# A two-block network kernel: states of the recurrence advanced from PSUM, the branch's gate a chunk ahead, and the moments' sums in PSUM

## The reference

```python
hx = modulate(rmsnorm(x, g_pre_mix[i]), sh1, sc1)
yx = token_mixers(hx @ w_in[i], s_f, s_b, rows, GRID_W, *gla_p, g_head[i], w_sc[i], b_sc[i])
x = x + gt1 * rmsnorm(yx @ w_out[i], g_post_mix[i])
hx = modulate(rmsnorm(x, g_pre_ffn[i]), sh2, sc2)
x = x + gt2 * rmsnorm(conv_ffn(hx, ...), g_post_ffn[i])

# token_mixers: a gated linear attention, forward and backward in time, beside a short convolution
o_gla = rmsnorm(o_f + o_b, g_head).reshape(bsz, t, GLA_WIDTH) * jax.nn.silu(og)
o_sc = sb * dwconv_row(sc * sx, w_sc, b_sc, rows, width)
return jnp.concatenate([o_gla, o_sc], axis=-1)

# one step of the recurrence of o_f and o_b
s_new = s * jnp.exp(b_last)[..., None] + jnp.einsum('bjhk,bjhv->bhkv', kc * jnp.exp(b_last[:, None] - b), vc)
```

## Time and profile before

| what | value |
|---|---|
| three executions | 1440.09, 1440.62, 1445.21 us |
| the profiled execution | 1444.85 us |
| its span | 1443.1 us |
| busy: TensorE, weight load, VectorE, ScalarE, GpSimd | 96%, 78%, 64%, 27%, 58% |
| TensorE's idle time | 59.8 us (span less 1383.3) |
| mean granted clock of TensorE | 0.972 of full speed |

### The profile page before, as it was taken

The page is one execution under the profiler, slowest core; times in us unless marked ns, Lnnn a source line. Parts: engine busy times, 40 slices in busy tenths (PEclk is TensorE's granted clock), DMA queues, the critical chain, the costliest instruction groups (busy, mean ns, idle before and its releaser), DMA issues.

```text
span 1443.1 us, 19746 instructions
## 1 busy us (share of the span) xinstructions
PE 1383.3 (96%) x6947; PEld 1123.8 (78%) x6947; DVE 929.6 (64%) x1305; ACT 391.7 (27%) x751; POOL 832.0 (58%) x651
## 2 busy tenths in 40 slices
PE   6999899989899999999999999999899999999998
PEld 4677678877788888888877888666688888888887
DVE  5696687756677777774038698735766888886000
ACT  3442223332222222201013202345413333332000
POOL 1343434425666666677746676432367777777775
PEclk9999999989799999999989999999999999999999
DMA  9456222112133333254322333211133333333332
GB/s 355 150 199 210 56 58 60 59 45 73 42 90 102 94 95 102 86 164 140 95 83 74 88 102 88 60 58 45 43 90 88 102 94 95 101 90 94 92 93 84
DMA packets 224459, 142.05 MB, mean 98 GB/s; under 512 B 5611, under 2 KB 211088, under 8 KB 224400
## 3 DMA queue, kind: packets, MB, share of 16 engines
q1 hardware_dynamic: 221333, 136.45, 31.7%
q10 hardware_dynamic: 3067, 4.78, 1.0%
HBM read 139.12 MB, written 2.10 MB: 98 GB/s over the span
## 4 chain that ended last, share of the span: by engine, by line
PE 84%; DVE 9%; issue 2%; ACT 2%; POOL 2%; DMA 0%; SPq 0%; DVEq 0%; POOLq 0%; ACTq 0%
PE ps L570 25%; PE ps L572 24%; PE ps L571 24%; PE ps L892 2%; DVE norm_acc L1751 1%; POOL w_lo L529 1%; PE ps L1174 1%; DVE ada_acc L1843 1%; PE ps L1145 1%; PE ps L1161 1%; DVE SS L2048 1%; PE ps L647 1%; DVE xT L2285 1%; POOL w_hi L526 1%; ACT h_hi L1259 1%
## 5 line engine op out<-in xcount | busy, mean ns | idle before, releaser
L529 POOL TENSOR_TENSOR w_lo<-raw,w_hi 128x1024 fp32r<-128x1024 f32 x212 | 531.2, 2505 | 17.7
L570 PE MATMUL ps<-h_hi,w_hi 128*128 128x512 f32 x1056 | 422.1, 400 | 8.6 <-DVE h_lo L2158 3.1
L572 PE MATMUL ps<-h_hi,w_lo 128*128 128x512 f32 x1056 | 414.0, 392 | 0.0
L571 PE MATMUL ps<-h_lo,w_hi 128*128 128x512 f32 x1056 | 413.8, 392 | 0.0
L525 POOL TENSOR_TENSOR w_hi<-raw,cst 128x16 fp32r<-128x16 f32 x212 | 64.9, 306 | 574.5 <-PE ps L572 517.1
L570 PEld LDWEIGHTS ps<-h_hi,w_hi 128*128 128x128 f32 x1056 | 199.6, 189 | 60.6 <-issue 14.0
L572 PEld LDWEIGHTS ps<-h_hi,w_lo 128*128 128x128 f32 x1056 | 199.6, 189 | 42.8
L571 PEld LDWEIGHTS ps<-h_lo,w_hi 128*128 128x128 f32 x1056 | 199.9, 189 | 39.2
L526 POOL TENSOR_SCALAR w_hi<-raw 128x1008 fp32r<-128x1008 f32 x212 | 229.2, 1081 | 0.0
L2203 DVE SCALAR_TENSOR_TENSOR f_acc<-ps,par,f_acc 128x441 f32<-128x441 f32 (+2 forms) x176 | 122.2, 694 | 27.2 <-ACT f_acc L1259 4.9
L570 PE MATMUL ps<-f_hi,w_hi 128*128 128x512 f32 x352 | 138.5, 393 | 0.9 <-POOL w_lo L529 0.8
(11 more groups left out here) (337 smaller groups left out, 2012.0 us busy)
## 6 DMA issues: line engine op xcount, KB each, us to landing
raw<-in_w_up SPq DMA_DIRECT2D x88, 512.0 KB, 3.7
raw<-in_w_in SPq DMA_DIRECT2D x59, 512.0 KB, 3.7
raw<-in_w_down SPq DMA_DIRECT2D x32, 512.0 KB, 3.6
ada_first<-in_w_ada SPq DMA_DIRECT2D x8, 1024.0 KB, 10.1
raw<-in_w_out SPq DMA_DIRECT2D x16, 512.0 KB, 3.5
v_tok<-in_w_ada SPq DMA_DIRECT2D x14, 512.0 KB, 5.2
raw<-in_w_down SPq DMA_DIRECT2D x16, 384.0 KB, 3.3
ada<-in_w_ada SPq DMA_DIRECT2D x10, 512.0 KB, 5.1
```

The source lines that it names most:

```text
L529: pool.tensor_tensor(w_lo[:, slot % 2, :], raw[:, slot, :], w_hi[:, slot % 2, :].bitcast(F32), ALU.subtract).then_inc(S("lo_split"), 1)
L570: nc.tensor.matmul(dst, lhs_hi, rhs_hi, start=first, stop=False)
L571: nc.tensor.matmul(dst, lhs_hi, rhs_lo, start=False, stop=False)
L572: return nc.tensor.matmul(dst, lhs_lo, rhs_hi, start=False, stop=last)
```

## The change

- The order of the states is context, context, 3, 0, 2, 1. Their products go to banks 5 and 6 in turn. ScalarE copies out three half products (keep_states), and VectorE advances a state in one step from its product in PSUM (advance, state): four instructions for a state, eight for the second. Of these, four groups come in the states' stage and before the first level, two in chunk 0 (state(5), first_backward) and one in chunk 1 (last_forward).
- The tanh of the output gate and its product with og are made at the end of the chunk before (branch_tanh, branch_gate), and for tile 0 among the states.
- In the last chunk three quarters of tiles 0, 1 and 2 follow levels 0, 1 and 2, their last quarters level 3, two halves of tile 3 levels 4 and 5, and tile 4 level 6 (MIX_EARLY). The attention's gate is applied a chunk at a time.
- The sums of squares and of weighed squares are in PSUM from tile 0 to 6, and one column group of matmuls after the last tile takes them (moment_columns_summed); no sum stands inside the last tile. The two last sums leave for SBUF at tile 6.
- The reciprocal of the second root (invert(3)) goes ahead of the wait for the first spread, and VectorE adds the residual of tile 0 (residual_first) in GpSimd's place.

```diff
-    STATE_ORDER = [CHUNKS, CHUNKS + 1, 0, 1, 2, 3]
+    STATE_ORDER = [CHUNKS, CHUNKS + 1, 3, 0, 2, 1]
...
-    MIX_BANKS = [0, 1, 2, 3, 7, 4, 5, 6]
-    CROSS_BANK, SQUARE_BANK, WEIGHED_BANK, MOMENT_BANK = MIX_BANKS[0:4]
+    MIX_BANKS = [0, 2, 3, 1, 7, 4, 5, 6]
+    CROSS_BANK, WEIGHED_BANK, SQUARE_BANK, MOMENT_BANK = MIX_BANKS[0:4]
...
+        def moment_columns_summed():
             pe.wait_ge(S("norm_added"), added(2, ADDS[2]))
             moment_sums(norm_acc, 0, const("mean"), True)
-            pe.wait_ge(S("weighed_added"), ADDED_TILES)
+            pe.wait_ge(S("weighed_added"), KT - 1)
             moment_sums(norm_root, 1, const("mean"))
-            pe.wait_ge(S("norm_squared"), squared(2, 6))
-            moment_sums(norm_sq[:, 0, :], 0, moment_columns[0])
-        def late_moments():
-            pe.wait_ge(S("cross_added"), CROSSED_TILES)
+            pe.wait_ge(S("norm_squared"), squared(2, KT - 1))
+            moment_sums(norm_sq[:, 1, :], 0, moment_columns).then_inc(S("norm_ss"), 1)
+            pe.wait_ge(S("cross_added"), KT - 1)
             cross_sums(norm_rinv, True)
-            pe.wait_ge(S("norm_squared"), squared(2, 7))
-            moment_sums(norm_sq[:, 1, :], 0, moment_columns[1]).then_inc(S("norm_ss"), 1)
             pe.wait_ge(S("cross_made"), KT - 1)
...
-                    pe.wait_ge(S("branch_act" if n == 2 else "branch_dve"), (3 * tile, 3 * tile, 2 * tile, 3 * tile - 2)[n] - (n == 0))
+                    done = (("gated_og", tile), ("branch_dve", 2 * tile), ("branch_act", 2 * tile), ("branch_dve", 2 * tile - 1))[n]
+                    pe.wait_ge(S(done[0]), done[1])
...
-            if n >= 1:
-                pe.wait_ge(S("state_read"), n)
+            if n == 2:
+                pe.wait_ge(S("state_kept"), 1)
+            elif n >= 3:
+                pe.wait_ge(S("state_added"), n - 2)
             keys = (g_qe, g_att)[n % 2]
             for h in range(GH):
-                mm = nc.tensor.matmul(ps[:, 5, h * P:(h + 1) * P], keys[:, h * P:(h + 1) * P],
+                mm = nc.tensor.matmul(ps[:, 5 + n % 2, h * P:(h + 1) * P], keys[:, h * P:(h + 1) * P],
...
-            pe.wait_ge(S("states_done"), CHUNKS)
+            pe.wait_ge(S("state_added"), 7 if c == CHUNKS - 1 else 6)
...
+        MIX_EARLY = [[(0, 0, 3)], [(1, 0, 3)], [(2, 0, 3)], [(0, 3, 4), (1, 3, 4), (2, 3, 4)], [(3, 0, 2)], [(3, 2, 4)], [(4, 0, 4)]]
+        def mix_early(n):
+            free = {0: ("gated_og", CHUNKS), 1: ("branch_act", 2 * CHUNKS), 2: ("branch_dve", 2 * CHUNKS - 1), 3: ("branch_dve", 2 * CHUNKS)}
+            for m, k0, k1 in MIX_EARLY[n]:
+                if k0 == 0 and m in free:
+                    pe.wait_ge(S(free[m][0]), free[m][1])
+                out_tile("out_s", m, ys_hi, ys_lo, 0, range(k0, k1))
         for c in range(CHUNKS):
             for n in range(LV):
                 level(c, n)
                 if c < CHUNKS - 1:
                     branch(c + 1, n)
-                elif n >= 2:
-                    if n == 2:
-                        pe.wait_ge(S("branch_act"), 2 * CHUNKS)
-                        pe.wait_ge(S("branch_dve"), 3 * CHUNKS)
-                    out_tile("out_s", n - 2, ys_hi, ys_lo, 0)
+                else:
+                    mix_early(n)
...
-        for m in range(KT - 1):
+        for m in range(KT):
             out_tile("out_g", m, yg_hi, yg_lo, 4)
-        out_tile("out_g", KT - 1, yg_hi, yg_lo, 4, range(0, 2))
-        early_moments()
-        out_tile("out_g", KT - 1, yg_hi, yg_lo, 4, range(2, 4))
-        late_moments()
+        moment_columns_summed()
...
+        def branch_tanh(i):
+            act.wait_ge(S("units_done"), FIRST["branch"] + 4 * i + 1)
+            activate(og[:, i, :], ps[:, 0, :], ACT.Tanh, scale=0.5).then_inc(S("branch_act"), 1)
...
+        def keep_states(n):
+            act.wait_ge(S("state_mm"), n + 1)
+            if n == 0:
+                activate(s_tmp[0:DK, :], ps[0:DK, 5, :], ACT.Copy)
+                activate(SS[DK:P, CHUNKS - 1, :], ps[DK:P, 5, :], ACT.Copy).then_inc(S("state_kept"), 1)
+            else:
+                activate(SS[0:DK, CHUNKS - 1, :], ps[0:DK, 5, :], ACT.Copy).then_inc(S("state_kept"), 1)
...
-            if n >= 2:
-                key_decay(n)
-            if n == ALL_CHUNKS - 1:
+            if 2 <= n + 1 < ALL_CHUNKS:
+                key_decay(n + 1)
+            if n == 1:
                 activate(small[:, 0:GH * ALL_CHUNKS].rearrange("p (h c) -> p h c", h=GH), dec[:, :, :], ACT.Exp,
                          scale=1.0 / TAU).then_inc(S("decay_ready"), 1)
+            if n in (1, 5):
+                keep_states(n - 1)
             act.wait_ge(S("ke_turned"), n + 1)
             if n >= 2:
                 act.wait_ge(S("state_mm"), n - 1)
             activate((g_qe, g_att)[n % 2][:, :], ps[:, 4 + 3 * (n % 2), :], ACT.Copy).then_inc(S("ket_copied"), 1)
+            if n == 3:
+                branch_tanh(0)
...
+        def advance(rows, dst, src, c, add):
+            for h in range(GH):
+                cols = slice(h * P, (h + 1) * P)
+                ins = vec.scalar_tensor_tensor(dst[rows, cols], src[rows, cols],
+                                               small[rows, h * ALL_CHUNKS + c:h * ALL_CHUNKS + c + 1],
+                                               add[rows, cols], ALU.mult, ALU.add)
+            return ins
...
+        def state(n):
+            new = ps[:, 5 + n % 2, :]
             dve.wait_ge(S("state_mm"), n + 1)
...
+            if n == 1:
+                dve.wait_ge(S("decay_ready"), 1)
+                dve.wait_ge(S("state_kept"), 1)
+                advance(up, SS[:, 0, :], s_tmp, CHUNKS + 1, new)
+                ins = advance(down, SS[:, 3, :], new, CHUNKS, SS[:, 3, :])
+            else:
+                dve.wait_ge(S("state_added"), n - 1)
+                if n == 2:
+                    ins = advance(down, SS[:, 2, :], SS[:, 3, :], 3, new)
+                elif n == 3:
+                    ins = advance(up, SS[:, 1, :], SS[:, 0, :], 0, new)
+                elif n == 4:
+                    ins = advance(down, SS[:, 1, :], SS[:, 2, :], 2, new)
+                else:
+                    ins = advance(up, SS[:, 2, :], SS[:, 1, :], 1, new)
+            ins.then_inc(S("state_added"), 1)
+        def first_backward():
+            dve.wait_ge(S("state_mm"), ALL_CHUNKS)
+            dve.wait_ge(S("state_added"), 4)
+            advance(down, SS[:, 0, :], SS[:, 1, :], 1, ps[:, 6, :]).then_inc(S("state_added"), 1)
+        def last_forward():
+            dve.wait_ge(S("state_kept"), 2)
+            dve.wait_ge(S("state_added"), 6)
+            advance(up, SS[:, 3, :], SS[:, 2, :], 2, SS[:, 3, :]).then_inc(S("state_added"), 1)
...
+            if n >= 3:
+                state(n - 2)
...
-        def head_gate(last):
-            tok = slice(T - P, T) if last else slice(0, T - P)
-            dve.wait_ge(S("head_scaled"), CHUNKS if last else CHUNKS - 1)
-            if not last:
-                dve.wait_ge(S("branch_dve"), 3 * CHUNKS)
+        def head_gate(c):
+            tok = slice(c * P, (c + 1) * P)
+            dve.wait_ge(S("head_scaled"), c + 1)
+            dve.wait_ge(S("gated_og"), CHUNKS)
...
+        state(4)
+        branch_gate(0)
+        dve.wait_ge(S("ke_turned"), ALL_CHUNKS)
...
-                if c == 0 and 2 <= n < 2 + CHUNKS:
-                    if n > 2:
-                        dve.wait_ge(S("states_done"), n - 2)
-                    advance_states(n - 2)
-                if n == 5 and c == CHUNKS - 1:
-                    head_gate(False)
+                if c == 0 and n == 0:
+                    state(5)
+                elif c == 0 and n == 2:
+                    first_backward()
+                elif c == 1 and n == 4:
+                    last_forward()
+                if n == 5 and c < CHUNKS - 1:
+                    branch_gate(c + 1)
+                if c == CHUNKS - 1 and n in (2, 4, 5):
+                    head_gate((0, 1, 2)[(2, 4, 5).index(n)])
...
+            if m < KT - 1:
                 dve.wait_ge(S("cross_made"), m)
                 dve.wait_ge(S("cross_added"), m)
-                vec.tensor_tensor(norm_rinv[:, :] if m == CROSSED_TILES - 1 else cross, cross, buffer, ALU.add).then_inc(S("cross_added"), 1)
+                vec.tensor_tensor(norm_rinv[:, :] if m == KT - 2 else cross, cross, buffer, ALU.add).then_inc(S("cross_added"), 1)
+        def square_of(m):
+            return norm_sq[:, m % 2, :] if m else norm_acc[:, :]
+        def squares_summed(m):
+            squares = ps[:, SQUARE_BANK, :]
+            dve.wait_ge(S("norm_squared"), squared(2, m))
+            if m == 0:
+                dve.wait_ge(S("cross_made"), 2)
+                vec.tensor_copy(squares, square_of(0)).then_inc(S("norm_added"), 1)
+                return
+            dve.wait_ge(S("norm_added"), added(2, m))
```

(24 more changed lines are left out.)

103 lines of the change are left out of this document (35 added, 68 removed).

## The result

The changed kernel takes 1420.93 us (median; 1417.56 to 1423.49), the kernel before 1440.62 (1439.82 to 1445.21), five runs each: ratio 0.9851, 95% interval 0.9831 to 0.9871. The forecast was 1420.5 with a range of 1412 to 1431. The profiled execution took 1418.89, its span is 1417.1.

The account below looks back on a forecast made before the run. TensorE, busy 96% of the span, was taken as the bound; gains of 1.3 + 6.3 + 5.7 + 6.8 = 20.1 us from the median 1440.62 gave 1420.5, own range 1415 to 1426, 8 in 10 from 1412 to 1431.

Parts of the forecast that it names:

- States: Stage before chunk 0: three keys ahead of the first advance save half of TensorE's 2.6 us of waits; gain 1.3.
- the first level's data: Start of chunk 0: TensorE's wait of 0.5 us for this data, counted within that chunk's 8.7 us of losses.
- Chunk 0: First chunk: 8.7 us of waits and slow stretches shrink to 2.4; gain 6.3, bounds 3 and 8.7.
- With og gated ahead, the level's start no longer waits for it.: Chunk 0, first level: making the og product earlier removes TensorE's wait for og, 2.3 us.
- The last chunk: Last chunk: earlier mixer matmuls fill the waits and keep the clock up; gain 5.7, bounds 4 and 7.5.
- the three gates: Last chunk: attention gates applied per chunk lengthen VectorE's chain between levels, 0.74 us each, costing 2.2 together.
- The moments: Mixer's last tiles to feed-forward: sums in PSUM, uninterrupted last tile (6.0) and earlier second reciprocal (0.8); gain 6.8.
- The lock: VectorE instructions with two SBUF inputs run longer beside GpSimd's w_lo; two moments sums would lose 3.9 us less.
- A: Rival: GpSimd holding VectorE, not the order, makes the waits of states and chunk 0; time 1425.8, chance 0.17.
- B: Rival: tail stays slow, all matmul groups at 1.84 us and VectorE 3.8 later; price 5.3, time 1425.8, chance 0.12.
- C: Rival: slower, short waits hold the clock low all through chunk 0 and the last chunk; time 1456.4, chance 0.04.
- D: Rival: better, the waits left in chunk 0, the last chunk, tail and states go too; time 1413, chance 0.04.

## Why the prediction was right, and where it was not

The experiments build the change up one part at a time. From the first key to the feed-forward: 229.96 before; the moments 221.93 (8.0); the last chunk 216.15 (5.8: 6.4 in the chunk itself, 0.7 more in chunk 0 by the early tanh, and 1.2 given back in a tail that is 14.16 after 12.99); the states 207.67 (8.5: 3.9 in their stage, 4.9 in chunk 0, 0.3 given back in the tail); og's product ahead 207.45 (0.2, nearly all of it in the tail). Together 22.5.

- **States.** Right in kind, too small: 1.3 forecast in that stretch and 0.5 for the first level's data, which stands at its end, against 3.8. I kept half of the waits because GpSimd would hold ke, and it does: one took 2.76 us beside a split, and two others 1.43 and 1.67. But the key was turned in time, since three keys ahead leave VectorE a whole half unit of the branch as cover. VectorE:

```profile
149.65 2.76 DVE L1926 TENSOR_TENSOR g_z<-g_e,p 64x512 f32<-64x512 f32 x1 [3.43 <-ACT g_e L1262]
```

  GpSimd's w_lo stands from 149.48 to 151.87 there. The waits of 2.6 and 0.5 are all gone; the last 0.7 is TensorE's busy time around them (25.79 to 25.07), which goes with the restarts.
- **Chunk 0.** The size was right and one step's reason was not. Counting without the 0.5, 34.2 was forecast and 34.39 measured, with no slow stretch. The waits left were put at 1.2, 0.3 and 0.9, and are 1.23, 0.18 and 1.31. The step that failed is "With og gated ahead, the level's start no longer waits for it." Of the wait of 2.27 us, the early tanh takes 0.5 (1.78 in the kernel with the old states and the gate late) and the new states 1.3 (0.50 in the kernel with the gate late); the last 0.5 is taken from level 1's wait. So of the 5.6 us of chunk 0, 4.9 come with the states, 0.7 with the tanh, and nothing with the product's move, which in the old states makes chunk 0 longer.
- **The last chunk.** 5.7 forecast, 6.4 measured. The early matmuls are worth 6.0 by the kernel without them. The term that was mis-sized is the three gates: 2.2 forecast, 0.6 measured. I had counted each gate's length and not what VectorE waits for beside it; two of them lie in its idle time. A wait that the forecast had no term for, 0.78 at level 4, made up for part of that, and the 0.3 put at level 1 did not come.
- **The moments.** 6.8 forecast, 6.7 between the two profiles, 8.0 alone. L2218, the counterpart of L2152, starts 11.4 us after the mixer's last matmul (11.2 forecast). Of the 6.7, 1.0 stands from the first spread on, where 0.8 was forecast. The lock was a reason for the rest, as said: with the sums in SBUF the tail is 9.2 longer. But that kernel keeps all the sums in SBUF, where the kernel before had three instructions with two SBUF inputs, and it loses more than the whole change gained. So it shows that the lock sets the tail, and not what share of the 5.7 it had; the last tile's uninterrupted run was not tried apart. The forecast allowed that COPY and TENSOR_SCALAR into PSUM be held; they took 0.68 and 0.74, the latter under a running w_lo. The Trainium skill, SBUF — State Buffer, Who interferes with whom, says that a VectorE instruction with at most one SBUF input, outside the two-port modes, does not contend with GpSimd, and the trace agrees for the TENSOR_SCALAR; no w_lo stood beside the COPY. The size is less certain than the two profiles suggest: with the same code the tail takes 12.99 to 15.20 us, as the clock falls in the third, fourth or fifth group.
- **Rivals.** A, the lock, sets two waits that are left and the long instructions above, but not the pace of the states. B is half true: the clock fell in the fourth group, as the earlier trace rows hinted, and the price was small since three groups were through. Its price of 5.3 was also added wrongly: 364.2 less 361.5 is 2.7, which with the 3.8 makes 6.5. The Trainium skill, TensorE: Matmul & The Clock Gate, Part 1, has activity release the higher level; the trace agrees so far, the clock falling in one-column groups (1.03 us, then 1.64 and 1.84) and staying low through both spreads. C did not come: chunk 0 and the last chunk stand at 1.00 in the changed kernel, yet its mechanism showed in three other profiles, for 1.5 us in two of them. D did not come either: waits of 2.7 us are left in chunk 0, and 1.4 in the last chunk.

The bare median gain, 19.7 us, is below the stretch's 22.5; the interval of the ratio, 18.6 to 24.3 us, holds both. So the forecast's 20.1 hit the median more closely than its parts deserve: it was 2.4 low on the stretches, and that the median came out at 1420.93 beside 1420.5 is in part luck.
